# ScalarE's split of weight panels moved to the head of each unit in four multilayer stages

## Chip, cores and metric

The kernel runs on one core of a Trainium2 chip. The metric is the device time of one execution in microseconds (us), median of the runs. Engines: TensorE (PE), VectorE (DVE), ScalarE (ACT), GpSimd (POOL) and SyncE (SP), each with a queue that it works off in the order written; semaphores join them.

## The reference, cut to what matters

Two blocks run one after the other on 512 tokens of width 1024, all float32. The second has two layers and carries 256 context tokens along. Each layer has a token mixer (attention, recurrence or convolution branches, gates) and a multilayer part, with RMS norms modulated by vectors that are matrix products of the conditions:

```python
def swiglu(h, w_gu, w_down):                 # first block, width 2816, twice (ffn1, ffn2)
    g, u = jnp.split(h @ w_gu, 2, axis=-1)
    return (jax.nn.silu(g) * u) @ w_down

def _sq_relu_mlp(h, w1, w2):                 # second block, width 4096, once a layer (mlp1, mlp2)
    return jnp.square(jax.nn.relu(h @ w1)) @ w2

mod = (c_act @ w_ada[l] + b_ada[l])          # modulation of every norm; likewise w_mod_2 for c and c_ctx
```

mlp1 works on 768 tokens (512 and the context), the other three stages on 512.

## The kernel before, in words

**Panels and their split.** All weights lie in device memory as panels of 128 x 2048 float32 (1 MB), 252 of them, in the order of use. SP loads them into two buffers (`raw`, line 548), panel p into buffer p % 2, as soon as POOL has read the panel two before (`lo_ready`). To keep float32 precision every product is three matmuls of fp32r parts: ACT copies the raw panel into a high part (`whi`, function `split`, L602), POOL subtracts it from the raw one in four quarters, which gives the low part (`wlo`, L561), and PE's helper `tri` (L1647 to L1649) multiplies high by high, high by low and low by high. `split(p)` waits for the load and for `panel_used` at p - 1, that is until PE is done with panel p - 2, whose `whi` buffer it takes. PE waits for `lo_ready` before it starts on a panel (`ups`, `down`) and raises `panel_used` behind its last matmul.

**A multilayer stage** (`mlp`) goes through the hidden width in chunks of 256: 11 in ffn1 and ffn2, 16 in mlp1 and mlp2. In chunk c PE computes the up product of chunk c and then the down product of chunk c - 1. In ffn1 and ffn2 (`gated`) the up product has two panels p and p + 1, one for each half (unit n = 0, 1) of the chunk, and the down product panel p + 2. In mlp1 and mlp2 the up product has one panel p, whose first half is announced by the semaphore `up_first` and the second by `panel_used`, and the down product panel p + 1. Each panel is 48 matmuls of 512 columns (in mlp1 the up panel has 48 of 512 and 48 of 256, the down panel 72 of 512).

**A unit n of a chunk.** ACT takes Silu or Relu of the product in PSUM (L689, L691), DVE multiplies by the other operand (L1192, L1195), ACT copies the result to the high part of the hidden (L697), DVE subtracts for its low part (L1198). The hidden of chunk c is needed by PE in chunk c + 1. PE's next product into the same PSUM banks waits for `hid`, DVE's product of the unit.

**The down product** has 8 outputs (12 in mlp1) of 128 x 512, six matmuls each, that go in turn through three PSUM banks (4, 5, 6). DVE adds each to y in SBUF (`add`, L1209, semaphore `added`), and PE's output o waits until the output three before it is added. In DVE's queue the additions of a chunk stand behind both units of that chunk.

**Modulation sums.** The modulation vectors are computed beside ffn1, ffn2 and mlp1. `mod_load` on ACT's queue (L610) waits until DVE has read the panel two before (`mod_read`) and loads 1 MB into one of the buffers `mraw`; DVE multiplies it by the conditions and sums (`mod`, L1101 once, L1104 seven times; from panel 36 on for two conditions, 16 instructions in all); PE adds over partitions behind the down product (`sums`). Each chunk from the first on has two such panels in ffn2 and mlp1 and in chunks 1 and 2 of ffn1, all before unit 0's product; chunks 3 to 10 of ffn1 have three, the third before unit 1's product. mlp1's chunk 15 and mlp2 have none.

**ACT's order before**, in `units(c, p)`, for each n: the chunk's `mod_load`s; `split(p + n + 1)` (ungated: only for n = 0); the wait for PE's product of the unit; the wait for `hid_lo` of the last chunk's unit; the activation; the wait for `hid`; the Copy. Behind both units stands `split(p + UP + 1)`, where UP is 2 in gated stages and 1 in the others: the first panel of the next chunk. `units` is called for chunk 0, for the `lead` chunks, in a hardware loop of two chunks a trip (where waits are counted in registers, `lin`), and for the `rest`.

Of the kernel before, what the change touches and what calls it, by code (L numbers as in the profile page):

```python
# [159 lines left out]
class Counts:  # L160
# [14 lines left out]
    def up(self, kind, key=None, by=1):  # L175
        s = self.sem(kind)
        self.count[kind] += by
        if key is not None:
            self.name(kind, key, kind, self.count[kind])
        return s, by  # L180
# [11 lines left out]
    def at(self, kind, key, plus=0):  # L192
        if self.known is None:
            return self.sem(kind), 1
        sem_kind, v = self.known[(kind, key)]
        out = v + plus
        assert not isinstance(out, int) or out > 0, (kind, key, plus)
        return self.sem(sem_kind), out
# [126 lines left out]
def program(nc, ctx, io, C, first, n_panels, stop):  # L325
# [120 lines left out]
    def wide(bank, T):  # L446

        return ps[:, bank:bank + len(spans(T)), :].rearrange("p a n -> p (a n)")[:, 0:T]

    def lin(a, b, i):  # L450

        return a if i is None else i * b + a
# [138 lines left out]
    def _(act):  # L591
        already_split = set()

        def split(p, i=None, by=0):

            if p >= n_panels or (i is None and p in already_split):
                return
            already_split.add(p)
            act.wait_ge(raw_loaded[p % 2], lin(16 * (p // 2 + 1), 8 * by, i))
            if p >= 2:  # L600
                act.wait_ge(panel_used, lin(p - 1, by, i))
            act.activation(whi[:, p % 2, :], raw[:, p % 2, :], ACT.Copy).then_inc(hi_ready, 1)  # L602

        def mod_load(k, i=None, by=0):

            if k < 10:
                act.wait_ge(mod_used, 8)
            else:
                act.wait_ge(mod_read, lin(k - 9, by, i))
            act.dma_start(mraw[:, k % 2, :], io["mod_panels"][lin(k, by, i)]).then_inc(mod_loaded[k % 2], 16)  # L610
# [10 lines left out]
        def gate_rows(st, banks):  # L621

            for g, _ in groups(NORMS[st][0][0]):
                b = banks[2 * g]
                act.wait_ge(*at("gate_sums", (st, g)))
                ins = act.activation(grow[:, g, :], ps[:, b:b + 2, :].rearrange("p a n -> p (a n)"), ACT.Copy)
                ins.then_inc(*up("gate_row", (st, g)))
            C.name("gate_rows", st, *C.labels[("gate_row", (st, g))])
# [41 lines left out]
        def mlp(m):  # L670
            st, T = m.name, m.T
            for kind in ("acted", "hid_hi"):
                C.start(kind, st)

            def units(c, p, i=None, mods=(0, 0)):

                for n in range(2):
                    for v in (range(2, mods[1]) if n else range(min(2, mods[1]))):
                        mod_load(mods[0] + v, i, 2 * m.half)
                    if m.gated or n == 0:  # L680
                        split(p + n + 1, i, m.per_trip)
                    if m.gated or n == 1:
                        act.wait_ge(panel_used, lin(p + (n if m.gated else 0) + 1, m.per_trip, i))
                    else:
                        act.wait_ge(*at("up_first", ("start", st), lin(c + 1, 2, i)))
                    if c >= 1:
                        act.wait_ge(*at("hid_lo", ("start", st), lin(2 * (c - 1) + n + 1, 4, i)))
                    if m.gated:
                        act.activation(tmp[:, n, 0:T], ps[:, 2 * n, 0:T], ACT.Silu).then_inc(*up("acted"))  # L689
                    else:  # L690
                        act.activation(tmp[:, n, 0:T], wide(2 * n, T), ACT.Relu).then_inc(*up("acted"))  # L691
                    act.wait_ge(*at("hid", ("start", st), lin(2 * c + n + 1, 4, i)))
                    if c >= 2:
                        act.wait_ge(panel_used, lin(down_panel(m, c - 2) + 1, m.per_trip, i))
                    elif i is not None:
                        act.wait_ge(panel_used, lin(p, m.per_trip, i))
                    act.activation(dhi[:, c % 2, n, 0:T], tmp[:, n, 0:T], ACT.Copy).then_inc(*up("hid_hi"))  # L697

            units(0, m.p0)
            for n in range(len(m.lead)):  # L700
                units(1 + n, m.panel(1 + n), mods=m.lead_mods(n))
                split(m.panel(1 + n) + m.UP + 1)
            with C.loop(act, m.trips) as i:
                for u in range(2):
                    p = m.panel(m.loop0 + u)
                    units(m.loop0 + u, p, i, m.loop_mods(u))
                    split(p + m.UP + 1, i, m.per_trip)
            for c in m.rest:
                units(c, m.panel(c))
                split(m.panel(c) + m.UP + 1)  # L710
            split(m.p0 + m.UP * m.C + m.C)
            gate_rows(AFTER[st], (0, 1, 2, 3))

# [356 lines left out]
        for n, st in enumerate(ORDER):  # L1070
            if st == "n0":
                norm_tail(st)
            elif st in NORMS:
                after_mix = ORDER[n - 1].startswith("mix")
                norm(st, (lambda t, st=st: keep_half(st, t, 1)) if after_mix else None)
            elif st in MLPS:
                mlp(MLPS[st])
            else:
                mix_act(st)
# [1141 lines left out]
def down_panel(m, c):  # L2221

    return m.p0 + m.UP * min(c + 2, m.C) + c
# [94 lines left out]
```

## Time and profile before

| what | us |
|---|---|
| median of 3 runs | 4394.3 |
| lowest and highest run | 4390.8, 12436.76 |
| the profiled execution | 4396.47 |
| its span, first to last instruction | 4394.6 |
| mean granted TensorE clock | 0.951 |
| PE, DVE, ACT, POOL busy in the span | 3955.3, 2291.2, 1368.4, 1333.8 |

The span is what the trace covers; the time of the execution is 1.9 us longer. The clock is given as a share of 2.4 GHz. PE's busy time overlaps itself, since matmuls are pipelined: a wait of PE is read from the starts of its matmuls. Of the stages, ffn1 lies at about 68 to 441 us, ffn2 at 941 to 1352, mlp1 at 2560 to 3137 and mlp2 at 4030 to 4386.

### The profile page before, as it was taken

The numbers are of one execution on the slowest core, as the hardware profiler recorded it, in microseconds if no ns is written. First come the engines' busy times: TensorE is split into PE (matmuls) and PEld (weight loads), VectorE is DVE, ScalarE is ACT, GpSimd is POOL, SyncE is SP. The second block draws the span as 40 slices with busy tenths as digits, with TensorE's granted clock in tenths as the row PEclk, the third lists the DMA queues.
The fourth block names the chain that finished last, engine by engine and source line by source line (L and its number), as shares of the span: only waits on it lengthen the run. The fifth ranks groups of instructions, "written<-read, shape, count | busy, mean of one in ns | idle before, by whom it ended". The sixth has DMA issues, their size and how long they took to land.

```text
span 4394.6 us, 50811 instructions
## 1 busy us (share of the span) xinstructions
PE 3955.3 (90%) x18628; PEld 3174.8 (72%) x18628; DVE 2291.2 (52%) x3495; ACT 1368.4 (31%) x1832; POOL 1333.8 (30%) x1012
## 2 busy tenths in 40 slices
PE   7999898989997979799879979999797889798999
PEld 6888676867776748558668768888674747577887
DVE  4676744146664361641682267777545352824334
ACT  3222643241214242252112341111424242224223
POOL 2444332433442103003232313322120303434443
PEclk8999999999998999899989989999998999899999
DMA  4454221223331102001111123332110202222222
GB/s 178 172 191 162 77 81 58 93 99 132 143 143 54 39 0 72 20 1 58 58 53 63 58 80 124 122 115 102 44 51 20 72 0 69 76 86 78 95 95 86
DMA packets 57220, 364.68 MB, mean 83 GB/s; under 512 B 5744, under 2 KB 12144, under 8 KB 13936
## 3 DMA queue, kind: packets, MB, share of 16 engines
q1 hardware_dynamic: 42064, 271.11, 17.7%
q10 hardware_dynamic: 15008, 91.49, 5.5%
q8 instruction: 105, 1.72, 0.2%
q14 instruction: 43, 0.35, 0.0%
HBM read 360.49 MB, written 2.10 MB: 83 GB/s over the span
## 4 chain that ended last, share of the span: by engine, by line
issue 68%; POOL 24%; PE 8%; POOLq 0%; DVE 0%; ACT 0%; DVEq 0%; ACTq 0%
POOL b_wlo L561 24%; PE ps L1647 3%; PE ps L1648 3%; PE ps L1649 3%; POOLq L575 0%; DVE b_y L1156 0%; POOLq L577 0%; DVE b_x L1160 0%; DVE b_y L1209 0%; PE ps L1732 0%; ACT b_whi L602 0%; PE ps L1719 0%; ACT b_xout L667 0%; DVE b_stat L1158 0%; POOLq L561 0%
## 5 line engine op out<-in xcount | busy, mean ns | idle before, releaser
L561 POOL TENSOR_TENSOR b_wlo<-b_raw,b_whi 128x512 fp32r<-128x512 f32 x1008 | 1333.6, 1355 | 3040.3 <-ACT b_whi L602 3040.3
L1647 PE MATMUL ps<-b_hhi,b_whi 128*128 128x512 f32 (+1 forms) x3000 | 1110.7, 370 | 42.1 <-DVE b_vp L1548 28.8
L1648 PE MATMUL ps<-b_hlo,b_whi 128*128 128x512 f32 (+1 forms) x3000 | 1101.1, 367 | 0.0
L1649 PE MATMUL ps<-b_hhi,b_wlo 128*128 128x512 f32 (+1 forms) x3000 | 1100.0, 367 | 0.0
L602 ACT ACTIVATE b_whi<-b_raw 128x2048 fp32r<-128x2048 f32 x252 | 480.9, 1908 | 752.1 <-PE ps L1649 735.5
L1647 PEld LDWEIGHTS ps<-b_hhi,b_whi 128*128 128x128 f32 x3000 | 569.6, 190 | 140.3 <-issue 38.6
L1648 PEld LDWEIGHTS ps<-b_hlo,b_whi 128*128 128x128 f32 x3000 | 569.5, 190 | 93.1 <-issue 2.0
L1649 PEld LDWEIGHTS ps<-b_hhi,b_wlo 128*128 128x128 f32 x3000 | 568.8, 190 | 93.5
L1104 DVE SCALAR_TENSOR_TENSOR b_macc<-b_mraw,b_csil,b_macc 128x256 f32<-128x256 f32 x868 | 506.1, 639 | 7.0
L1209 DVE TENSOR_TENSOR b_y<-ps,b_y 128x512 f32<-128x512 f32 x496 | 335.6, 689 | 274.0 <-PE ps L1649 274.0
L1647 PE MATMUL ps<-b_whi,b_dhi 128*128 128x512 f32 x992 | 400.2, 403 | 53.9 <-POOL b_wlo L561 28.1
L1648 PE MATMUL ps<-b_wlo,b_dhi 128*128 128x512 f32 x992 | 395.8, 399 | 0.0
L1649 PE MATMUL ps<-b_whi,b_dlo 128*128 128x512 f32 x992 | 394.2, 397 | 0.0
L1647 PEld LDWEIGHTS ps<-b_whi,b_dhi 128*128 128x128 f32 x992 | 190.4, 192 | 110.8 <-DVE b_y L1209 37.5
L1568 DVE SCALAR_TENSOR_TENSOR b_cv<-b_vp,b_par,b_cv 128x512 f32<-128x512 f32 (+1 forms) x270 | 233.1, 891 | 5.9
L1461 DVE TENSOR_REDUCE b_small<-ps 128x1 f32<-128x768 f32 (+1 forms) x160 | 135.0, 849 | 167.5 <-PE ps L2058 156.4
L1649 PEld LDWEIGHTS ps<-b_whi,b_dlo 128*128 128x128 f32 x992 | 190.5, 192 | 42.5
L1648 PEld LDWEIGHTS ps<-b_wlo,b_dhi 128*128 128x128 f32 x992 | 190.7, 192 | 39.3
L1437 DVE TENSOR_TENSOR b_gate<-ps,b_gate 128x768 f32<-128x768 f32 (+1 forms) x48 | 39.5, 823 | 261.4 <-PE ps L1649 261.1
L908 ACT ACTIVATE b_pr<-ps,b_small 128x768 f32<-128x768 f32 (+1 forms) x160 | 130.1, 813 | 103.5 <-DVE b_small L1461 103.5
L697 ACT ACTIVATE b_dhi<-b_tmp 128x512 fp32r<-128x512 f32 (+1 forms) x108 | 75.1, 695 | 238.8 <-DVE b_tmp L1195 151.8
L892 ACT ACTIVATE b_gate<-ps 128x768 f32<-128x768 f32 (+1 forms) x64 | 45.1, 705 | 315.0 <-PE ps L1649 315.0
(289 smaller groups left out, 5005.7 us busy)
## 6 DMA issues: line engine op xcount, KB each, us to landing
b_raw<-panels SPq DMA_DIRECT2D x252, 1024.0 KB, 4.7
b_mraw<-mod_panels ACTq DMA_DIRECT2D x78, 1024.0 KB, 6.6
b_y<-mod_panels ACTq DMA_DIRECT2D x3, 1024.0 KB, 15.8
b_xin<-xT SPq DMA_DIRECT2D x1, 2048.0 KB, 25.4
b_mraw<-mod_panels SPq DMA_DIRECT2D x2, 1024.0 KB, 19.0
b_rope<-rope ACTq DMA_DIRECT2D x4, 512.0 KB, 3.3
outT<-b_xout SPq DMA_DIRECT2D x4, 512.0 KB, 3.6
b_mod<-mod_panels ACTq DMA_DIRECT2D x1, 1024.0 KB, 20.9
```

The costliest lines, as they stand in the source:

```text
L561: ins = pool.tensor_tensor(wlo[:, s, c], raw[:, s, c], whi[:, s, c].bitcast(F32), ALU.subtract)
L602: act.activation(whi[:, p % 2, :], raw[:, p % 2, :], ACT.Copy).then_inc(hi_ready, 1)
L697: act.activation(dhi[:, c % 2, n, 0:T], tmp[:, n, 0:T], ACT.Copy).then_inc(*up("hid_hi"))
L892: act.activation(gate2[:, t, 0:T], wide(2 * t % 4, T), ACT.Sigmoid).then_inc(*up("gate", X(tag, j, t)))
L908: act.activation(pr2[:, r % 2, rows.slot(j), 0:k1 - k0], s, ACT.Exp, bias=small[:, c:c + 1], accum_out=small[:, c + 4:c + 5]).then_inc(*up ...
L1104: ins = dve.scalar_tensor_tensor(acc, w, s, acc, ALU.mult, ALU.add)
L1209: dve.tensor_tensor(dst, ps[:, 4 + o % 3, :], dst, ALU.add).then_inc(*up("added"))
L1461: dve.tensor_reduce(small[:, c:c + 1], s, AX.X, ALU.max, negate=True).then_inc(*up("nmax", X(rows.tag, r, j)))
L1568: ins = dve.scalar_tensor_tensor(cv[:, a:b], tap, w, cv[:, a:b], ALU.mult, ALU.add)
L1647: pe.matmul(out, a[0], b[0], start=first, stop=False)
L1648: pe.matmul(out, a[0], b[1], start=False, stop=False)
L1649: return pe.matmul(out, a[1], b[0], start=False, stop=last)
```

## The change

ACT's splits in `units` are put elsewhere; nothing else is touched. Each chunk now begins with `split(p + 1)`, ahead of its `mod_load`s. Behind the wait that tells that PE has finished an up panel, and ahead of the activation, stands the split of the panel that takes its buffer: p + 2 in unit 0 and p + 3 in unit 1 of the gated stages, p + 2 in unit 1 of the others; in chunk 0 only the one of the gated unit 0. The splits behind the units (`p + UP + 1`) are gone, being the same panels as these.

```diff
--- before.py
+++ after.py
@@ -674,13 +674,14 @@
 
             def units(c, p, i=None, mods=(0, 0)):
 
+                split(p + 1, i, m.per_trip)
                 for n in range(2):
                     for v in (range(2, mods[1]) if n else range(min(2, mods[1]))):
                         mod_load(mods[0] + v, i, 2 * m.half)
-                    if m.gated or n == 0:
-                        split(p + n + 1, i, m.per_trip)
                     if m.gated or n == 1:
                         act.wait_ge(panel_used, lin(p + (n if m.gated else 0) + 1, m.per_trip, i))
+                        if c >= 1 or (m.gated and n == 0):
+                            split(p + (n if m.gated else 0) + 2, i, m.per_trip)
                     else:
                         act.wait_ge(*at("up_first", ("start", st), lin(c + 1, 2, i)))
                     if c >= 1:
@@ -699,15 +700,12 @@
             units(0, m.p0)
             for n in range(len(m.lead)):
                 units(1 + n, m.panel(1 + n), mods=m.lead_mods(n))
-                split(m.panel(1 + n) + m.UP + 1)
             with C.loop(act, m.trips) as i:
                 for u in range(2):
                     p = m.panel(m.loop0 + u)
                     units(m.loop0 + u, p, i, m.loop_mods(u))
-                    split(p + m.UP + 1, i, m.per_trip)
             for c in m.rest:
                 units(c, m.panel(c))
-                split(m.panel(c) + m.UP + 1)
             split(m.p0 + m.UP * m.C + m.C)
             gate_rows(AFTER[st], (0, 1, 2, 3))
```

## Rows read from the trace of the kernel before

**Rows 1.** Windows, four stages: us, PE, PEld, DVE, ACT, POOL busy, clock, DMA share, GB/s

```profile
68.00:441.00 373.00, 368.77 (x1663) 302.99 (x1662) 245.27 (x364) 90.59 (x81) 166.43 (x127) 0.99 0.46 166
941.00:1352.00 411.00, 379.89 (x1702) 312.02 (x1701) 255.44 (x462) 92.80 (x86) 171.30 (x132) 0.96 0.36 135
2560.00:3137.00 577.00, 557.47 (x2890) 472.80 (x2890) 427.56 (x733) 123.39 (x119) 168.80 (x128) 0.99 0.30 109
4030.00:4386.00 356.00, 351.54 (x1560) 289.57 (x1559) 143.84 (x213) 109.23 (x114) 161.66 (x128) 1.00 0.25 89
```

**Rows 2.** Waits: whole span, then 1040 to 1340 (total, times, longest)

```profile
PE ps L1647 <- POOL b_wlo L561: 36.1, 18, 8.4
...
PE ps L1647 <- POOL b_wlo L561: 14.7, 8, 1.9
```

**Rows 3.** Timeline of PE in mlp2 (start, us)

```profile
4203.10 0.39 PE L1647 MATMUL ps<-b_whi,b_dhi 128*128 128x512 f32 x1
...
4207.22 0.39 PE L1647 MATMUL ps<-b_whi,b_dhi 128*128 128x512 f32 x1
```

**Rows 4.** Timeline of ACT in mlp2

```profile
4203.30 0.60 ACT L691 ACTIVATE b_tmp<-ps 128x512 f32<-128x512 f32 x1 [3.46 <-PE ps L1649]
```

**Rows 5.** Timeline of DVE in mlp2

```profile
4205.31 0.69 DVE L1198 TENSOR_TENSOR b_dlo<-b_tmp,b_dhi 128x512 fp32r<-128x512 f32 x1 [0.70 <-ACT b_dhi L697]
4205.92 1.28 DVE L1209 TENSOR_TENSOR b_y<-ps,b_y 128x512 f32<-128x512 f32 x2
```

**Rows 6.** Timeline of ACT in mlp1, one chunk

```profile
2720.91 1.91 ACT L602 ACTIVATE b_whi<-b_raw 128x2048 fp32r<-128x2048 f32 x1 [12.52 <-PE ps L1649]
...
2739.66 0.80 ACT L691 ACTIVATE b_tmp<-ps 128x768 f32<-128x768 f32 x1
...
2742.02 0.34 ACTq L610 DMA_DIRECT2D b_mraw<-mod_panels  x1
```

**Rows 7.** Timeline in ffn2, DVE and POOL at once

```profile
984.32 1.22 DVE L1198 TENSOR_TENSOR b_dlo<-b_tmp,b_dhi 128x512 fp32r<-128x512 f32 x1 [0.69 <-ACT b_dhi L697]
...
982.50 4.17 POOL L561 TENSOR_TENSOR b_wlo<-b_raw,b_whi 128x512 fp32r<-128x512 f32 x3 [14.63 <-ACT b_whi L602]
```

**Rows 8.** Timeline of PE in mlp1, the same chunk

```profile
2744.14 0.50 PE L1647 MATMUL ps<-b_whi,b_dhi 128*128 128x512 f32 x1 [0.64 <-DVE b_y L1209]
```

**Rows 9.** Tile b_mraw from 2740 to 2760

```profile
DMA to landing us min/median/max: 4.7/5.7/6.6
```

**Rows 10.** Timeline of DVE in mlp1, the same chunk

```profile
2722.13 9.81 DVE L1104 SCALAR_TENSOR_TENSOR b_macc<-b_mraw,b_csil,b_macc 128x256 f32<-128x256 f32 x14
...
2732.38 5.63 DVE L1104 SCALAR_TENSOR_TENSOR b_macc<-b_mraw,b_csil,b_macc 128x256 f32<-128x256 f32 x14
...
2743.40 1.88 DVE L1209 TENSOR_TENSOR b_y<-ps,b_y 128x512 f32<-128x512 f32 x3
```

**Rows 11.** Timeline of ACT, then DVE, in ffn1

```profile
217.08 0.60 ACT L689 ACTIVATE b_tmp<-ps 128x512 f32<-128x512 f32 x1 [7.02 <-PE ps L1649]
...
218.55 0.68 DVE L1192 TENSOR_TENSOR b_tmp<-b_tmp,ps 128x512 f32<-128x512 f32 x1
...
220.53 1.88 DVE L1209 TENSOR_TENSOR b_y<-ps,b_y 128x512 f32<-128x512 f32 x3
...
237.13 3.61 DVE L1104 SCALAR_TENSOR_TENSOR b_macc<-b_mraw,b_csil,b_macc 128x256 f32<-128x256 f32 x7
```

**Rows 12.** Timeline of ACT in ffn2

```profile
1093.85 0.63 ACT L697 ACTIVATE b_dhi<-b_tmp 128x512 fp32r<-128x512 f32 x1 [4.41 <-DVE b_tmp L1192]
```

**Rows 13.** Windows as in rows 1 (ffn2, ffn2, mix2), and PE in mix2

```profile
1063.70:1067.10 3.40, 3.40 (x10) 2.62 (x9) 1.18 (x2) 1.56 (x1) 1.76 (x2) 0.50 0.80 267
1040.00:1340.00 300.00, 285.33 (x1273) 234.39 (x1271) 194.77 (x348) 62.64 (x56) 124.91 (x96) 0.97 0.35 133
1500.10:1504.00 3.90, 3.90 (x6) 2.15 (x7) 1.05 (x2) 0.00 (x0) 0.00 (x0) 0.50 0.00 0
...
1500.10 2.05 PE L2057 MATMUL ps<-b_dk,b_qm 128*128 128x512 f32 x2 [5.16 <-DVE b_qm L1451]
```

## The prediction

> **What bounds the kernel now.** I read the stage windows first. In the four multilayer stages TensorE (PE) is busy for 99, 92, 97 and 99% of the stretch [rows 1]; the reader is to see that nothing else is near that in mlp2 and that VectorE (DVE) comes next. So a change pays or costs there only by what it does to the waits of PE. Then the list of waits. Over the whole span PE waits 36.1 us for a low part of a panel (L561), in 18 places, and 14.7 us of it, 8 waits of 1.9, stand in the steady part of ffn2 [rows 2]. That is all that an earlier split can win directly. Then I follow one chunk of each stage on ScalarE (ACT), DVE and PE. The resource to look at is the ring of three PSUM banks of the down product: eight outputs (twelve in mlp1) go through it, six matmuls each, and the fourth has to wait until DVE has added the first to y. DVE does these additions behind both units of the next chunk and behind that chunk's modulation sums, so whatever makes ACT or DVE late in a chunk sits in front of them.
>
> mlp2 shows it bare. D is the first matmul of the down panel, 4203.10, and the fourth output starts at 4207.22, D+4.12 [rows 3]. ACT begins the second Relu at D+0.20 [rows 4], and DVE ends the first addition at 4205.92+0.69 = 4206.61, D+3.51 [rows 5]. There are 0.6 us to spare.
>
> **1. The split in front of the second activation.** It issues no new instruction: the same L602 (1.91 us [rows 6]) stands before the activation instead of after the Copy. The path activation, product, Copy, low part of the hidden (L1198), addition is serial, so the first addition ends 1.9 later, D+5.4. The bank is due at D+4.1: 1.3 us of wait. In front of the first activation the same move costs nothing: that unit's result is wanted only a panel later (48 matmuls of 0.229, 11 us).
>
> **2. What the earlier split drags with it.** POOL's low part now begins at about D+2.2 and runs 5 us, over the L1198 that used to run before it. Trace: L1198 takes 0.69 alone [rows 5] and 1.22 where POOL was at work [rows 7]. I take 0.5 us for each 512-wide one. In mlp1 the L1198 comes 2.9 after its Relu, just after POOL's third quarter has begun; I take 0.9 there (bounds 0 and 1.3, one quarter).
> The Trainium skill (SBUF — State Buffer, Who interferes with whom) says that a VectorE instruction with two SBUF inputs and a GpSimd one that reads SBUF exclude each other for the whole instruction, whoever comes first. The 1.22 us row agrees. By the rule a worst phase would cost a whole quarter every time, some 0.8 us more per chunk in mlp2, 12 us in all; by the row it is 0.5.
>
> A wait that is ended by such an addition costs about 0.2 more on PE: in mlp1 the matmul after it takes 0.50 and its gap is 1.04 where the wait is 0.64 [rows 8]. So mlp2 loses 1.3+0.5+0.1 = 1.9 us in each of 15 chunks: **+29 us**.
>
> **3. The loads of the modulation panels.** This is the part that the words of the change do not name. Before, ACT issues them at the end of a chunk, before it waits for anything (2742.02 [rows 6]); they land 4.7 and 6.6 us later [rows 9], long before DVE has done its last addition and starts on them (first L1104 at 2722.1 [rows 10]). Now split(p+1) comes first in the unit, its wait for `panel_used` ends only when the down panel is finished (S = 2720.91 in mlp1 [rows 6]), and the two loads are queued on ACT behind it. They go out at S+0.2 and S+0.8 and land at S+4.9 and S+7.4. DVE starts 4.2 us later than now.
> Half of that comes back. A modulation pair now starts in the shadow of POOL: its 14 L1104 take 9.81 us against 5.63 for the second pair [rows 10], 4.2 us lost. When it starts at S+5, POOL has 2.3 of its 5.2 us left: 1.8 lost. Without a lock a pair is 5.63 and 0.5 for its two first products, 6.1. So DVE is through at S+5.0+2x6.1+1.8 = S+19.0 instead of S+17.1 (2732.38+5.63).
>
> **4. mlp1.** In order from there: product and Copy of unit 0 (now the second Relu is at S+18.75 [rows 6], 1.7 after the sums) S+20.8, split to S+22.7, Relu. From Relu to the end of the first addition it is 2743.40+0.68-2739.66 = 4.4 [rows 6, 10]: S+27.1, and 0.9 for the lock, S+28.0. Now it is 2744.1, S+23.2. So +4.8 us per chunk, all of it PE's, since PE already waits 0.8 at this place [rows 8]. Chunks 2 to 14: 13 x 4.8 = 62. Chunk 1 has its loads late already and gets +2.9; chunk 15 has no sums and gets 1.9+0.9 = 2.8. **+68 us**.
>
> **5. ffn1.** D = S+23.0 (96 matmuls of 0.229 and 1 us of modulation matmuls). Loads land at S+4.9 and 7.4; two sums of 4.0 us each (3.61 and 0.4 [rows 11]) with some 2.6 of lock end at S+15.5. The third load is issued behind the Copy, S+16.4, lands at S+21.3, and its sum of 4.0 us, with one quarter of POOL's next low part over its end, is done near S+26.4; product to addition is 2.7 (218.55 to 221.2 [rows 11]) and the lock 0.5: S+29.6 against S+27.1 due, with 0.2 for the restart 2.7 lost. Today the first addition ends 221.2, with the panel begun about 0.2 before the Silu of 217.08, D+4.3: 0.4 lost. So +2.3 in each of eight chunks, 18; the chunk with two sums +2; the first chunk wins: its low part is late today too (3.4 us of the 36.1 [rows 2], an estimate of mine from the chunk's ACT order), and the clock falls behind it: -4. **+16 us**.
>
> **6. ffn2.** Today ACT waits 4.4 us for DVE before the Copy of 1093.85 [rows 12], since DVE is in the sums; the split stands behind it, and PE waits 1.9 for the low part [rows 2]. With the split at S+12.7, behind the first up panel, that wait is gone. But POOL then works over the second pair of sums: S+5.0+12.2+1.8+4.2 = S+23.2 instead of S+17. Copy S+24.5, split 26.4, Silu to addition 3.3, lock 0.5: S+30.2 against a bank due at S+27.5. With the restart 2.9 lost in place of 2.1: +0.8 x 9 = 7; the first chunk, which today waits 8.4 us [rows 2] but would then wait some 6 for its bank, -2. **+5 us**. The gain of the change is exchanged for the bank wait.
>
> **7. The clock.** Behind a wait the records show 0.50 (1.2 GHz, the lower level) in stretches such as 1063.7 to 1067.1, 10 matmuls in 3.4 us; at 2.4 GHz 15 start in it (0.229 each in mlp2 [rows 3]), so one costs 1.6 us. In ffn2 the mean over eight waits of 1.9 is 0.97: 300x0.03/0.5 = 17 us at the lower level, five such stretches, about one in every second chunk. Waits of 0.8 leave mlp1 at 0.99. After a wait of 5.2 us at 1500.10 the clock is 0.50 for the next 3.9 us, 2 us lost [rows 13]. mlp1's waits become 5.6 us: 13x2.0 and 1 more = 27 (bounds 10 and 50). ffn1's become 2.5: 8x1.0 = 8. ffn2's: +3. mlp2's become 1.8: between 0 (as at 0.8) and 15x0.8 = 12; I take 4. **+42 us**.
>
> Sum: 29+68+16+5+42 = 160 on the profiled execution's 4396.5 (its span is 4394.6): 4556. The median of the runs shown is 2 us lower, so **4554 us**, +3.6%.
>
> **Rivals.**
> A, the panels win and the rest hides (ends on the other side). It would be so if the banks came free in time: the deciding point is a first addition before D+4.1. Then ffn2's 2.1 a chunk (19), its clock (7), its first chunk (10) and ffn1's first (6) are won: 4394-42 = 4352. For it: DVE is busy only 40 to 74% of the stages [rows 1]. Against: mlp2's chain has 0.6 us to spare and gets 1.9. 3%.
> B, the loads' delay hides and only the split in front and the lock count: mlp2 33, mlp1 15x2.8 plus some 20 of clock 62, ffn1 20, ffn2 0: 4510. For it: DVE stands idle while the up products run in mlp2 and ffn1. Against: in mlp1 and ffn2 the sums fill DVE until the product. 17%.
> C, as forecast, but the clock costs little: nothing behind waits of 1.8 to 2.9 us and 1 us behind those of 5.6: 160-15-13, so 4526. It lies inside the forecast's own range.
> D, the clock stays low through the down panel after each 5.6 us wait, 4 us each instead of 2: +26, 4580; with locks at their upper bound 4600. 14%. For it: the 3.9 us [rows 13] are no upper limit. Against: PE is then busy without a break for the rest of the panel.
>
> **Chances.** Forecast with C 66%, A 3%, B 17%, D 14%. About 2% (88 us) is what a measurement of this kernel tells from no change; the line lies at 4482. Faster 1%, same 10% (most of A, and B with small clock costs and locks), slower 89%. The range runs from B without half its clock, 4485, to D, 4600.
>
> **What would show it.** In the profile after: the wait of PE for b_wlo falls from 36 us to a few; that of PE for DVE's L1209 appears in mlp2 (15 times, 1.5 to 2 us) and grows in mlp1 to 5 us; DVE's L1101 waits some 4 us for its load in each of over 30 chunks; L1198 is 1.2 us long in mlp2; PEclk drops below 1 inside mlp1. It is wrong if mlp2's chunks stay at 21.9 us, or if L1101 still starts right behind the last addition.

## The result and the profile after

The changed kernel takes 4520.25 us (median of 4 runs, 4512.37 to 4524.98) beside 4395.72 for the kernel before: a ratio of 1.028, 95% interval 1.027 to 1.029. It is slower by 125 us. The kernel before took 12436.76 us in one slow run of its four, which the ratio leaves out. The profiled execution has a span of 4523.0 us (4394.6 before) and a mean granted clock of 0.944 (0.951). 4520 is 34 us below the forecast of 4554, inside its range, and 6 us from rival C.

In after, the lines of DVE and PE have numbers two lower than in before (L1209 is L1207, L1198 is L1196, L1104 is L1102, L1101 is L1099, L1647 is L1645) and the activations' numbers one higher (L691 is L692, L697 is L698). L602, L610 and L561 keep theirs.

First the stage windows of after, which answer to [rows 1]. Columns: stretch, length, busy time and count of PE, weight loads, DVE, ACT and POOL, then PEclk, DMA share and GB/s. The stretches are ffn1, ffn2, mlp1 and mlp2:

```profile
68.00:451.00 383.00, 365.23 (x1637) 299.80 (x1636) 221.59 (x362) 87.25 (x77) 168.91 (x126) 0.99 0.45 162
955.00:1354.00 399.00, 374.42 (x1696) 305.43 (x1695) 242.06 (x459) 93.68 (x88) 216.17 (x131) 0.99 0.38 139
2564.00:3232.00 668.00, 586.40 (x2881) 494.40 (x2880) 406.77 (x728) 120.67 (x116) 171.10 (x128) 0.92 0.25 94
4127.00:4514.00 387.00, 355.65 (x1557) 287.71 (x1556) 150.88 (x214) 109.12 (x115) 167.63 (x128) 1.00 0.23 81
```

PE fell from 97% of the stretch to 88% in mlp1, where the clock fell to 0.92 as well, and from 99% to 92% in mlp2. ffn1 loses less, and ffn2 is 12 us shorter, not longer. The list of waits over the whole span says for what (columns: total us, times, longest), first of before, then of after:

```profile
PE ps L1647 <- DVE b_y L1209: 25.4, 19, 7.8
```


```profile
DVE b_macc L1099 <- DMA b_mraw<-mod_panels: 173.3, 42, 6.0
...
PE ps L1645 <- DVE b_y L1207: 138.7, 52, 10.0
...
PE ps L1645 <- POOL b_wlo L561: 19.6, 17, 4.4
```

PE's wait for the low part, 36.1 us in [rows 2], is down by 16.5. Its wait for DVE's addition has grown by 113.3, from 19 places to 52.

**mlp2.** One chunk on ACT, DVE and PE, to be read against [rows 3 to 5]:

```profile
4243.48 1.91 ACT L602 ACTIVATE b_whi<-b_raw 128x2048 fp32r<-128x2048 f32 x1 [3.51 <-PE ps L1647]
4245.30 0.58 ACT L692 ACTIVATE b_tmp<-ps 128x512 f32<-128x512 f32 x1
```

```profile
4247.30 1.25 DVE L1196 TENSOR_TENSOR b_dlo<-b_tmp,b_dhi 128x512 fp32r<-128x512 f32 x1 [0.70 <-ACT b_dhi L698]
4248.47 0.68 DVE L1207 TENSOR_TENSOR b_y<-ps,b_y 128x512 f32<-128x512 f32 x1
```

```profile
4243.14 0.39 PE L1645 MATMUL ps<-b_whi,b_dhi 128*128 128x512 f32 x1
...
4249.20 0.50 PE L1645 MATMUL ps<-b_whi,b_dhi 128*128 128x512 f32 x1 [1.78 <-DVE b_y L1207]
```

D, the first matmul of the down panel, is 4243.14. The split is now ahead of the Relu, the low part of the hidden takes 1.25 us instead of 0.69, and the first addition ends at 4249.15, D+6.0, 0.05 before the matmul that waited for it.

**mlp1.** The same engines in one chunk. The down panel is finished at S = 2705.04, where the split begins:

```profile
2705.04 1.91 ACT L602 ACTIVATE b_whi<-b_raw 128x2048 fp32r<-128x2048 f32 x1 [18.21 <-PE ps L1647]
2705.25 0.94 ACTq L610 DMA_DIRECT2D b_mraw<-mod_panels  x2
...
2725.53 1.90 ACT L602 ACTIVATE b_whi<-b_raw 128x2048 fp32r<-128x2048 f32 x1
2727.34 0.79 ACT L692 ACTIVATE b_tmp<-ps 128x768 f32<-128x768 f32 x1
```

```profile
2710.17 2.10 DVE L1099 TENSOR_SCALAR b_macc<-b_mraw,b_csil 128x256 f32<-128x256 f32 x2 [4.35 <-DMA b_mraw<-mod_panels]
...
2718.26 5.62 DVE L1102 SCALAR_TENSOR_TENSOR b_macc<-b_mraw,b_csil,b_macc 128x256 f32<-128x256 f32 x14
...
2730.02 2.02 DVE L1196 TENSOR_TENSOR b_dlo<-b_tmp,b_dhi 128x768 fp32r<-128x768 f32 x1 [0.91 <-ACT b_dhi L698]
2731.96 1.87 DVE L1207 TENSOR_TENSOR b_y<-ps,b_y 128x512 f32<-128x512 f32 x3
```

```profile
2732.69 0.80 PE L1645 MATMUL ps<-b_whi,b_dhi 128*128 128x512 f32 x1 [5.12 <-DVE b_y L1207]
```

The two loads (L610) go out at S+0.2, DVE begins at S+5.1, its sums end at 2723.88 = S+18.8, and PE goes on at S+27.7 after a wait of 5.12, where [rows 8] have 0.64. The matmul takes 0.80 us, and those that follow 0.63: the clock is at its lower level.

The program's time, stage by stage, in the profiled execution of each kernel. A stage is taken from the first to the last activation of its units, and a chunk from one such activation to the same one of the next chunk (the steady value; two where they alternate):

| kernel | ffn1 | ffn2 | mlp1 | mlp2 | chunks in this order |
|---|---|---|---|---|---|
| before | 347.9 | 379.0 | 531.9 | 320.4 | 34.4; 36.7, 38.2; 35.9; 21.9 |
| after | 357.7 | 366.6 | 623.8 | 351.5 | 36.2; 36.6; 42.1, 43.2; 23.9 |
| change | +9.8 | -12.4 | +91.9 | +31.1 | |
| forecast, with the clock | +24 | +8 | +95 | +33 | |
| loads first | 357.5 | 369.2 | 592.3 | 352.8 | 36.2; 36.6; 38.6 to 41.3; 23.9 |
| loads held | 358.3 | 403.7 | 562.0 | 320.4 | 36.2; 41; 37.6, later 39.1; 21.9 |
| gated first unit | 338.0 | 350.0 | 531.8 | 320.3 | 34.4; 34.5; 35.9; 21.9 |

The last three rows are the first three experiments. The four changes of after sum to 120.4; the other 8.0 of the 128.4 between the spans lie outside these bounds, 4.1 of them between ffn1's last activation and ffn2's first, where one more wait of PE (1.79) and one more fall of the clock (3.4 us at 0.50) stand. A stage's time is that of one execution: the profiled one of loads first is the fastest of its four (4485.83), that of the gated first unit the slowest of its four (4362.51).

### The profile page after: what moved, and what is told of

The parts are those of the page before. It is cut to its first block, busy times and chain, and to the rows that moved or that the text cites. A ratio compares the mean times of both kernels' runs of the same rounds, so it can differ in the third digit from the quotient of the medians.

```text
span 4523.0 us, 50773 instructions
## 1 busy us (share of the span) xinstructions
PE 3986.8 (88%) x18628; PEld 3188.6 (70%) x18628; DVE 2247.1 (50%) x3495; ACT 1367.9 (30%) x1832; POOL 1392.0 (31%) x1012
## 4 chain that ended last, share of the span: by engine, by line
issue 67%; POOL 23%; PE 8%; DVE 1%; POOLq 0%; ACT 0%; DVEq 0%; ACTq 0%
POOL b_wlo L561 23%; PE ps L1645 3%; PE ps L1646 3%; PE ps L1647 3%; DVE b_y L1207 0%; POOLq L575 0%; DVE b_y L1154 0%; POOLq L577 0%; DVE b_x L1158 0%; ACT b_whi L602 0%; PE ps L1730 0%; PE ps L1717 0%; DVEq L1202 0%; PE ps L1668 0%; DVEq L1205 0%
## 5 line engine op out<-in xcount | busy, mean ns | idle before, releaser
L561 POOL TENSOR_TENSOR b_wlo<-b_raw,b_whi 128x512 fp32r<-128x512 f32 x1008 | 1391.7, 1412 | 3110.6 <-ACT b_whi L602 3110.6
L1645 PE MATMUL ps<-b_hhi,b_whi 128*128 128x512 f32 (+1 forms) x3000 | 1110.1, 370 | 42.4 <-DVE b_vp L1546 28.8
L1647 PE MATMUL ps<-b_hhi,b_wlo 128*128 128x512 f32 (+1 forms) x3000 | 1099.7, 367 | 0.0
L602 ACT ACTIVATE b_whi<-b_raw 128x2048 fp32r<-128x2048 f32 x252 | 481.8, 1912 | 1236.3 <-PE ps L1647 1136.6
L1645 PEld LDWEIGHTS ps<-b_hhi,b_whi 128*128 128x128 f32 x3000 | 569.4, 190 | 140.3 <-issue 38.8
L1647 PEld LDWEIGHTS ps<-b_hhi,b_wlo 128*128 128x128 f32 x3000 | 568.5, 190 | 93.3
L1645 PE MATMUL ps<-b_whi,b_dhi 128*128 128x512 f32 x992 | 412.9, 416 | 150.0 <-DVE b_y L1207 138.7
L1207 DVE TENSOR_TENSOR b_y<-ps,b_y 128x512 f32<-128x512 f32 x496 | 331.9, 686 | 267.4 <-PE ps L1647 267.4
L1646 PE MATMUL ps<-b_wlo,b_dhi 128*128 128x512 f32 x992 | 405.3, 409 | 0.0
L1647 PE MATMUL ps<-b_whi,b_dlo 128*128 128x512 f32 x992 | 402.9, 406 | 0.0
L1102 DVE SCALAR_TENSOR_TENSOR b_macc<-b_mraw,b_csil,b_macc 128x256 f32<-128x256 f32 x868 | 377.7, 490 | 7.0
L1645 PEld LDWEIGHTS ps<-b_whi,b_dhi 128*128 128x128 f32 x992 | 196.6, 198 | 219.0 <-DVE b_y L1207 161.7
L1647 PEld LDWEIGHTS ps<-b_whi,b_dlo 128*128 128x128 f32 x992 | 196.3, 198 | 44.6
L1196 DVE TENSOR_TENSOR b_dlo<-b_tmp,b_dhi 128x512 fp32r<-128x512 f32 (+1 forms) x108 | 136.1, 1260 | 82.3 <-ACT b_dhi L698 82.3
L1099 DVE TENSOR_SCALAR b_macc<-b_mraw,b_csil 128x256 f32<-128x256 f32 x124 | 79.4, 671 | 173.3 <-DMA b_mraw<-mod_panels 173.3
```

The source lines that it names most:

```text
L561: ins = pool.tensor_tensor(wlo[:, s, c], raw[:, s, c], whi[:, s, c].bitcast(F32), ALU.subtract)
L1099: ins = dve.tensor_scalar(acc, w, s, None, ALU.mult)
L1102: ins = dve.scalar_tensor_tensor(acc, w, s, acc, ALU.mult, ALU.add)
L1196: dve.tensor_tensor(dlo[:, c % 2, n, 0:T], tmp[:, n, 0:T], dhi[:, c % 2, n, 0:T].bitcast(F32), ALU.subtract).then_inc(*up("hid_lo"))
L1207: dve.tensor_tensor(dst, ps[:, 4 + o % 3, :], dst, ALU.add).then_inc(*up("added"))
L1645: pe.matmul(out, a[0], b[0], start=first, stop=False)
```

## Experiments

Diffs are against the kernel before where nothing else is said. The first four take the change apart: the loads put back in their old place, the loads alone held behind the wait, the split of the gated first unit alone, and the split in front of the second activation in mlp2 alone. "The lock" is what an instruction of DVE loses while one of POOL keeps it from SBUF, or the other way round.

### The loads first again

```diff
(against the changed kernel)
-                split(p + 1, i, m.per_trip)
                 for n in range(2):
                     for v in (range(2, mods[1]) if n else range(min(2, mods[1]))):
                         mod_load(mods[0] + v, i, 2 * m.half)
+                    if n == 0:
+                        split(p + 1, i, m.per_trip)
```

> The changed kernel with one thing undone: the loads of the modulation panels go out before the first split of a chunk again, both other splits stay ahead of the activations. Theory T (two separate costs: loads held behind the split's wait, and the split in front of the second activation with POOL's lock): in mlp1 the sums end at S+17.1 again, the first addition at about S+26.0 instead of 27.9, so the bank wait falls from 5.9 to about 3.9 us and the chunk from 42.6 to about 40; mlp2 keeps its 23.95 us chunks. Time 4480 to 4495, about 30 less than the changed kernel. Rival R1 (the loads' place does not matter, since DVE catches up): within 5 us of the changed kernel, 4520. Rival R2 (all of mlp1's loss is the loads): mlp1 chunks at 36, time about 4430.

Measured: 4495.04 us, ratio 1.0233 (1.0216 to 1.025) to a before of 4394.38, at the upper edge of what was expected. Giving the loads their place back wins 25 us. The gain is mlp1's: 623.8 to 592.3. mlp1 keeps +60 from the split in front of the second Relu, the lock and a clock that is low for 61 us in 11 places (before: 10 us in one); rival B's price for the same, 15 x 2.8 and 20 of clock, was 62. ffn1 gains nothing: its third load, issued behind the first unit, is late in either order.

### The loads held, and nothing else

```diff
+                split(p + 1, i, m.per_trip)
                 for n in range(2):
                     for v in (range(2, mods[1]) if n else range(min(2, mods[1]))):
                         mod_load(mods[0] + v, i, 2 * m.half)
-                    if m.gated or n == 0:
+                    if m.gated and n == 1:
                         split(p + n + 1, i, m.per_trip)
```

> The kernel before with only one part of the change: split(p+1) stands ahead of the chunk's modulation loads, all other splits stay where they were. Theory T: the sums of mlp1 end 1.9 us later and so does the first addition, bank wait 0.8 to 2.7 us in 14 chunks, 27 us and some 10 of clock; in ffn2 the split behind the sums is later by the same 1.9, 17 us; ffn1 a few us: 4440 to 4460. mlp2 unchanged (21.9 us a chunk). R1: no difference to before, 4395. R2: 4480 or more, since then the loads explain the whole of mlp1.

Measured: 4461.05 us, ratio 1.0148 (1.0132 to 1.0165). Only the order of the first split and the loads is changed: two DMA issues of 0.34 us (L610) a chunk now stand behind a wait. The price is 67 us, at the upper edge of what was expected, since ffn2 lost 24.7 instead of 17 and ffn1 10.4 instead of a few. That shows the third part of the forecast by itself, and refutes rival B (the delay hides). In mlp1 it and the experiment before add up: +30.1 and +60.4 make 90.5, and after has +91.9. In ffn2 they do not: -9.8 and +24.7, but -12.4 together. Before, ffn2's low part had to wait until DVE was through its sums (the split stood behind the Copy, and the Copy behind DVE), so late loads made it later; with the split ahead of the first Silu it no longer does. In ffn1 either alone costs what both cost (+9.6, +10.4, +9.8). With the split in front, DVE is through its third sum before the second Silu starts (251.15 and 251.45 in after), so the delay of the loads has room, and PE waits 1.73 in after and 1.74 with the loads first. With the loads held alone PE loses 0.55 and 1.16 in the same chunk (before: 0.50), the second behind a third sum that ends only at 253.8.

### Only the gated first unit

```diff
-                    if m.gated or n == 0:
+                    if n == 0:
                         split(p + n + 1, i, m.per_trip)
                     if m.gated or n == 1:
                         act.wait_ge(panel_used, lin(p + (n if m.gated else 0) + 1, m.per_trip, i))
+                        if m.gated and n == 0:
+                            split(p + 2, i, m.per_trip)
```

> The kernel before with only the harmless part of the change: in the gated stages the split of panel p+2 goes ahead of the first unit's Silu; loads and all other splits as before. T: PE's waits for b_wlo in ffn2 (2 us a chunk and 8.5 in the first) and the low clock behind them go, 25 to 40 us; mlp1 and mlp2 unchanged; ffn1 gains 5 in its first chunk and loses up to 1.5 a chunk in its eight chunks with a third load, which is issued behind this unit: 4355 to 4380. Rival R3 (every split ahead of an activation costs): ffn2's chunks stay above 37 us, time 4400 to 4430.

Measured: 4354.27 us (4352.98 to 4362.51), just under the expected range, ratio 0.9909 (0.9892 to 0.9925). **It beats both kernels**, by 40 us and by 166. It is the one place of the change where an activation can wait: the hidden half that it makes is wanted only behind the whole second up panel. ffn2 runs at 34.5 a chunk, as ffn1 does, and its clock drops go from five to one. What remains of PE's waits for the low part (36.1 in [rows 2]):

```profile
PE ps L1649 <- POOL b_wlo L561: 13.3, 8, 5.1
```

### Only the second unit, in mlp2

```diff
                         act.wait_ge(panel_used, lin(p + (n if m.gated else 0) + 1, m.per_trip, i))
+                        if st == "mlp2" and c >= 1:
+                            split(p + 2, i, m.per_trip)
...
-                    split(p + m.UP + 1, i, m.per_trip)
+                    if st != "mlp2":
+                        split(p + m.UP + 1, i, m.per_trip)
```

> The kernel before with the split ahead of the second activation in mlp2 alone. T: mlp2 as in the changed kernel, 23.95 us a chunk, of its 2.05 us 1.9 by the split and the rest by POOL over L1198: +31, 4426 to 4428; all other stages as before. If stages act on each other (clock, tail), the sum differs from 31 by more than 3 us.

Measured: 4427.06 us, ratio 1.007 (1.0054 to 1.0087), +33 as expected; a chunk takes 23.9 instead of 21.9, and one 25.5 with a fall of the clock. mlp2 has no modulation load, so this is the first two parts of the forecast alone. The low part of the hidden:

```profile
4223.23 1.25 DVE L1201 TENSOR_TENSOR b_dlo<-b_tmp,b_dhi 128x512 fp32r<-128x512 f32 x1 [0.70 <-ACT b_dhi L699]
```

### How much of it is the lock: POOL in eighths, and in one piece

To the kernel of the last experiment, for mlp2's panels alone:

```diff
-            for q in range(4):
-                c = slice(q * PANEL // 4, (q + 1) * PANEL // 4)
+            for q in range(pieces):
+                c = slice(q * PANEL // pieces, (q + 1) * PANEL // pieces)
...
+            pieces = 8 if st == "n7" else 4      # 1 in the second kernel
```

> As e4_mlp2_only (split ahead of the second activation in mlp2 alone), but POOL makes the low part of mlp2's panels in eight pieces of 256 columns (about 0.65 us each) instead of four of 512 (1.29). Theory L (L1198 waits for the POOL instruction that is running, to its end): L1198 falls from 1.26 us towards 0.7 to 0.9, the chunk from 23.95 to 23.4 to 23.6 us, and the time by 5 to 8 us against e4, 4420. Rival (the 0.5 us come from somewhere else, such as the restart of PE): no change, 23.95.

> As e4_mlp2_only, but POOL makes the low part of mlp2's panels in one instruction of 2048 columns (about 5 us). L: L1198 waits to its end, some 3.3 us, the first addition is 2.5 us later than in e4, the chunk near 26.4 us, the time 35 to 40 above e4, 4465. Rival (DVE and POOL only share a bandwidth): L1198 stays near 1.26 us and the chunk at 23.95.

Measured: 4423.46 us (ratio 1.0069, 1.0046 to 1.0092) and, in two runs, 4479.47 (1.0193, 1.0137 to 1.0248). A chunk takes 23.5 and 27.4. The program's time does not show the gain of the eighths: it is 32.7 above its before in this kernel and in the one of the last experiment, with intervals of 7 to 10 us either way. The chunk shows it. DVE's instruction in the first and in the second, and POOL's in the second:

```profile
4215.47 0.85 DVE L1204 TENSOR_TENSOR b_dlo<-b_tmp,b_dhi 128x512 fp32r<-128x512 f32 x1 [0.70 <-ACT b_dhi L702]
```

```profile
4222.04 3.27 DVE L1204 TENSOR_TENSOR b_dlo<-b_tmp,b_dhi 128x512 fp32r<-128x512 f32 x1 [0.70 <-ACT b_dhi L702]
```

```profile
4220.21 4.55 POOL L563 TENSOR_TENSOR b_wlo<-b_raw,b_whi 128x2048 fp32r<-128x2048 f32 x1 [6.40 <-ACT b_whi L605]
```

0.85, 1.25 and 3.27 us for pieces of 256, 512 and 2048: DVE ends 0.55 after POOL's whole instruction (4225.31 against 4224.76), nearly the 0.69 that it takes alone. So it waited for the piece that had begun, to its end. The Trainium skill (SBUF — State Buffer, Who interferes with whom) says so: whichever of the two issues first keeps the shared ports for the whole instruction. The trace agrees here. The chunk follows by the same amounts in the first kernel (-0.4 for -0.40). In the second it grows by 3.5 for 2.0; the rest is the clock, which the expectation had left out:

```profile
4060.00:4430.00 370.00, 318.47 (x1288) 256.84 (x1288) 144.53 (x165) 82.16 (x79) 120.06 (x27) 0.93 0.21 77
```

In this window of mlp2 (columns as in the stage windows) the trace has 14 stretches at 0.50, 51 us together; half of that is lost, some 1.8 us a chunk. Waits of 3.8 us, 2 longer than those of after, brought the clock down in every one of the 15 chunks; those of after did so in none of mlp2.

### What decides between DVE's sums and POOL in ffn2

The sixth part of the forecast held that POOL's first quarters would push DVE's second pair of sums back by 4.2 us. In after it is the other way round. DVE, then POOL, in one chunk of ffn2 with S = 1081.1 (S as in mlp1, the moment at which the down panel is finished):

```profile
1088.24 5.63 DVE L1102 SCALAR_TENSOR_TENSOR b_macc<-b_mraw,b_csil,b_macc 128x256 f32<-128x256 f32 x14
1093.79 0.60 DVE L1099 TENSOR_SCALAR b_macc<-b_mraw,b_csil 128x256 f32<-128x256 f32 x2
1094.32 5.62 DVE L1102 SCALAR_TENSOR_TENSOR b_macc<-b_mraw,b_csil,b_macc 128x256 f32<-128x256 f32 x14
1099.86 0.67 DVE L1190 TENSOR_TENSOR b_tmp<-b_tmp,ps 128x512 f32<-128x512 f32 x1
```

```profile
1095.94 5.15 POOL L561 TENSOR_TENSOR b_wlo<-b_raw,b_whi 128x512 fp32r<-128x512 f32 x1 [7.77 <-ACT b_whi L602]
```

DVE's 14 instructions keep their 5.62 us, and POOL's first quarter, 1.29 us when nothing holds it, takes 5.15: it ends 1.15 behind the sums (1099.94 = S+18.8, not S+23.2), as if it had begun where they end. The same stands in all nine chunks of after's ffn2 from the third on (5.15 to 5.24). Elsewhere, as in [rows 10], the same two kinds of instruction take turns, and DVE's 14 need 9.8. Two readings were tried. P: it hangs on the moment, within one DVE instruction, at which POOL's arrives. Q: the stream that is already running keeps the ports. Four kernels move the arrival, each from the gated first unit, in ffn2 only. The first two put one or two one-column copies (into a column that nothing else reads at that time) in front of the split; the others cut the split into two and four instructions:

```diff
                         if m.gated and n == 0:
+                            for e in range(2 if st == "ffn2" else 0):    # 1 in the first kernel, into column 95
+                                act.activation(small[:, 94 + e:95 + e], eps[:, :], ACT.Copy)
                             split(p + 2, i, m.per_trip)
```

```diff
+            for q in range(parts):               # in ffn2's split(p + 2): 2 in the third kernel, 4 in the fourth
+                w = slice(q * PANEL // parts, (q + 1) * PANEL // parts)
+                ins = act.activation(whi[:, p % 2, w], raw[:, p % 2, w], ACT.Copy)
+            ins.then_inc(hi_ready, 1)
```

> As e3_gated_first_unit, with one ACT instruction of a single column (some 0.2 us) ahead of ffn2's split of panel p+2, so that POOL comes that much later into DVE's sums. In e3 the first quarter of this low part takes 3.4 us in every chunk while DVE's L1102 go on at 0.47 us. Theory P (the phase within DVE's stream decides who holds the port): in this kernel or in the next POOL gets in, its first quarter is 1.3 us and DVE's sums beside it 1.5 us each. Theory Q (the stream that has run longer keeps the port): POOL's first quarter stays above 3 us in both. Time as e3 within 10 us, since the chunk has slack for either: 4350 to 4365.

> As e7_late_by_one with two such instructions (some 0.4 us, about one sum of DVE). P: the other outcome than e7, or that of e3 again since the phase is nearly a full turn; Q: POOL's first quarter above 3 us. Time 4350 to 4365.

> As e3_gated_first_unit, with ffn2's split of panel p+2 made in two ACT instructions of 1024 columns, so that POOL comes some 0.1 to 0.2 us later into DVE's sums (the single-column instructions of e7 and e8 had moved it by under 0.05 us). In e3, e7 and e8 POOL came 0.16 to 0.21 us after the start of one of DVE's sums, which start every 0.40, and starved for 3.4 us; in the kernel before it came 0.34 to 0.40 after one and got in. P (phase decides): at about 0.35 POOL's first quarter is 1.3 us and the L1102 beside it 1.5 us. Q (the older stream keeps the port): it stays above 3 us. Time 4350 to 4365 in either case.

> The same in four instructions of 512 columns, some 0.4 to 0.6 us later than e3: P: starved or not by the phase that this makes, read from the starts (under 0.25: starved; 0.34 and more: not). Q: above 3 us less the delay. Time 4350 to 4365.

Measured, one run each: 4356.46 and 4358.72 us, then 4359.63 and 4355.96 (before: 4390.75 and 4390.22); none differs from the 4354 of the gated first unit by what one run can tell. With the gated first unit alone POOL's low part arrives 0.11 to 0.21 us after the start of a DVE instruction. The copies were of little use: one moved that by 0.01 us, two by 0.05 to 0.10. The cut splits moved it to 0.20 to 0.30, and to 0.38 in every second chunk and 0.04 after the next start in the others. POOL's first quarter was held every time, 3.2 to 3.5 us (9.3 to 9.6 in the stage's first chunk with sums). In the same kernels the low part of the other up panel arrives 0.34 to 0.38 us after such a start, with only two of the pair's 14 sums begun before it, and gets in every time. Both in the third kernel:

```profile
1061.05 1.29 POOL L561 TENSOR_TENSOR b_wlo<-b_raw,b_whi 128x512 fp32r<-128x512 f32 x1 [3.95 <-ACT b_whi L604]
```

```profile
1073.96 3.36 POOL L561 TENSOR_TENSOR b_wlo<-b_raw,b_whi 128x512 fp32r<-128x512 f32 x1 [7.32 <-ACT b_whi L604]
```

0.38 us gives both outcomes, so P falls. The trace of after says the same: it has arrivals at 0.35 to 0.39 in every second chunk and at 0.01 to 0.04 in the others, behind four or five instructions of the second pair's sums, and all are held. Q fits all of these arrivals, but no run varied how long the stream had been running with all else equal, so what decides stays open. It costs little: with POOL held for 3.4 to 3.5 us ffn2 has its best chunk, 34.5.

## Why the prediction was right, part by part

- **Parts 1 and 2, mlp2, +29.** Right. Forecast 1.9 a chunk, measured 2.07 (23.94 - 21.87), 31 in 15 chunks. The first addition was forecast at D+5.9 with the lock and ends at D+6.0 (4249.15 - 4243.14 = 6.01), since the split begins 0.34 after D where the Relu had begun 0.20 after it. The lock was put at 0.5 and is 0.56. mlp2's own runs show the two terms: eighths take 0.4 of the 2.07 away.
- **Part 3, the loads.** Right: DVE begins at S+5.1 (forecast S+5), loses 1.5 beside POOL on its first two products (2.10 - 0.60; forecast 1.8), its sums end at S+18.8 (S+19.0), and holding the loads alone costs 67 us.
- **Part 4, mlp1, +68, and its 27 of the clock.** Right: a chunk grew by 6.75 (the mean of 42.1 and 43.2, less 35.9), forecast 6.8. Of this 4.5 is the wait: from the last matmul ahead of it (2727.17) to the first behind it PE loses 5.29 beyond one matmul's 0.23, and lost 0.82 before; forecast 4.8. The rest, 2.3, is the clock, forecast 2.0: it is at 0.50 for 6.8 us in every one of chunks 2 to 14, of which 3.9 or 6.1 lie behind the wait's end. The lock was 1.06 (2.02 - 0.96), forecast 0.9.
- **Part 5, ffn1, +16.** Nearly: +1.8 a chunk for +2.3, since the third sum ends 0.5 before POOL's next low part begins and no lock falls on it; the first two chunks win 1.4 and 4.4, forecast 4 in one; the first fall of the clock is gone with them. In sum +9.8, where the forecast with its clock had 24.
- **Part 6, ffn2, +5.** **This step failed**, in its "S+5.0+12.2+1.8+4.2 = S+23.2". The 4.2 of lock fell on POOL instead of DVE. The low part then came late by 0.8 to 0.9 (PE waited 0.76 at 1105.40) and the bank wait was 0.71 instead of 2.7. Together, with the restarts, some 2.0 us a chunk are lost, as before the change, where 0.8 more was forecast. But one loss of 2 became two of 1, and the clock stayed up:

```profile
1000.00:1330.00 330.00, 316.80 (x1445) 258.47 (x1443) 207.79 (x396) 71.78 (x63) 177.86 (x108) 1.00 0.39 143
```

  Before, this stage had 5 stretches at 0.50 with 23.8 us; after it has one of 3.4. So in place of +8 came -12.4: 7 from the loss that did not grow, 3 from clock that was not lost, and about 10 from clock that came back (half of the 20.4 us less at the lower level).
- **Part 7, the clock, +42.** Right for mlp1 (27 forecast, 2.3 x 13 = 30 measured), too high elsewhere: 15 were put on ffn1, ffn2 and mlp2, whose waits of 0.7 to 1.8 us cost little (in mlp2 and ffn2's steady part no fall, in ffn1 two). Rival C was right on those and wrong on the long ones (1 us where 2.3 was lost); that its 4526 lies so near the result is in part that ffn2, which it had as forecast, came out lower. The forecast took ffn2's rows of before as the measure (a drop in every second chunk behind 1.9 us); mlp2 has waits as long (1.78) and no drop in 15 chunks. Two of the forecast's own figures are off without changing it: 300x0.03/0.5 is 18, not 17 (the trace has five stretches of 3.4, which is 17), and a stretch costs 1.5 (38.2 - 36.7), not 1.6.

The sum: 160 forecast. ffn2 came out 20 lower, ffn1 14, mlp1 3 and mlp2 2, which makes 40; the 8.0 outside the stages, which the forecast did not have, go against it, and 128 is what the spans differ by. So the parts that carry the result, mlp1 and mlp2, were right in mechanism and size, and that the total is off by 34 and not 40 is luck. Rival A priced the part that wins at 42, 4352 in all, and the gated first unit alone measured 4354. In its parts that is less exact: ffn1 won 9.9 where it had 6, ffn2 29.0 where it had 36.

## What to carry to other kernels

An instruction that is moved ahead of another pays its own length to all that stands behind it on its engine: before moving it, ask of each follower when its result is wanted, and move it only where that is later than its length (here unit 0 of the gated stages, a whole panel of slack, 40 us won; unit 1, 0.6 us of slack, 33 lost in mlp2 alone). A wait that is moved to the head of a queue holds what costs nothing itself: two DMA issues of 0.34 us a chunk behind it cost 67 us, so let loads go out before the engine waits. And a loss that is cut into shorter waits can be cheaper than the same loss in one: ffn2's 2 us in one wait brought the clock down in every second chunk, in two waits of 0.7 to 0.8 in none.

## What the runs showed of the hardware

- Of DVE's sums and POOL's subtraction now one, now the other gives way: in mlp1's [rows 10] they take turns and 14 sums take 9.8 us, in ffn2 after the change POOL's first quarter lost 3.9 us (5.15 - 1.29) while every sum kept its pace. One instruction keeping the ports to its end explains a hold of one instruction, 0.4 us, not one of ten sums.
- The clock's fall did not go by the wait alone. Waits of 1.9 us in ffn2 before brought it down in every second chunk, and waits of 1.8 in mlp2, at chunks of 23.9, in none of 15 in after and in one in the experiment on mlp2 alone. Waits of 1.7 to 1.8 in ffn1 in after, at chunks of 36.2, brought it down behind two of ten, so the length of the chunk alone does not decide either. Waits of 3.8 us, with POOL in one piece, brought it down in all 15 chunks for 3.6 us on the mean, and those of 5.1 in mlp1 in every steady chunk for 6.8 us. In mlp1 it fell 0.6 to 3.1 us before the wait ended, so a part of each fall cost nothing.
